# A two-block transformer on one core: Winograd's 2x2 products in a conv mixer, exchanged rope halves and scaled probabilities in attention, and other borders between stages

## The chip, the cores and the metric

One core of one Trainium2 chip. The metric is device time in microseconds of one launch, the median of three runs. TensorE runs at 1.2 or 2.4 GHz as the chip grants it; the profile calls full speed 1.0. Everything is computed in fp32. One fp32 matmul of the program is two MATMUL and two LDWEIGHTS instructions in the trace; a transpose is one of each.

## What is computed

The first block (windowed attention, a linear recurrence and a chunked RWKV part over 1024 tokens, with a layer norm) is not touched by the change. Behind it stands a second block of two layers over T = 1040 tokens (16 meta tokens and 1024) of width 1024:

```python
def short_conv_mixer(hn, w_in, conv_w, w_out):
    bcu = hn @ w_in                      # 1024 -> 3 x 1024
    b, c, u = jnp.split(bcu, 3, axis=-1)
    z = causal_conv(c * u, conv_w)       # 3 taps, each channel for itself
    return (b * z) @ w_out
# layer 0: h += short_conv_mixer(rmsnorm(h));  h += moe(rmsnorm(h))
# layer 1: cq = rmsnorm(rmsnorm(h) @ w_dq);  q = cq @ w_uq       (8 heads: 128 nope + 64 rope)
#          k_nope, v = rmsnorm(h' @ w_dkv) @ w_ukv;  k_rope shared by the heads
#          rope(x) = [x1 cos - x2 sin, x1 sin + x2 cos]
#          p = softmax(causal(q k^T * scale));  h += (p v) @ w_o;  h += moe(rmsnorm(h))
# out = rmsnorm(h) without the meta tokens
# moe: 8 groups x 8 experts, the two best experts of the best group for each token,
#      y = sum gate * (silu(x w_gate) * (x w_up)) w_down,  D_EXPERT = 256
```

## The kernel before

Each stage is one function with a `Phase` (L60 on), which owns buffers and semaphores, and in it one `nc.Block()`, in which each engine has its own written-out program; semaphores order them. A block ends with a DRAIN on each engine and a barrier. The exit of a phase (L76 on) clears the phase's semaphores and has another all-engine barrier (L80, L81). So nothing of the next stage begins before the slowest engine of the last is through. Order: `front`, the windowed attention, the RWKV chunks, `first_out`, `conv_mixer` (L1465), `back_and_route` and `experts` of layer 0 (both inside `moe`, L2750), `combine_and_latents` (L2376), `heads` (L1544), `moe` of layer 1, `combine_out` (L2650). `program_parts` (L2782) nests them. Weights of the next stage are loaded by SyncE (SP) at the end of a stage's program (`next_loads`).

`conv_mixer`: activations lie transposed, channels on partitions, as 8 k-tiles of 128 channels x 1040 tokens (`hnT`). For each of the 8 output tiles j and each of 3 cuts of the tokens (352, 352, 336) TensorE makes the three products b, c and u with 8 k-tiles each (L1505). ScalarE copies b and c out (L1520, L1521), VectorE multiplies c and u into z (L1533), and behind the last cut of a j come three taps (L1536, L1538) and the multiplication with b (L1541). TensorE is at most two cuts ahead of both (`z_made`, `copied`). Weights are 1.5 MB per j in a ring of two.

`heads` works on the 8 heads in 4 pairs. Per pair there are 14 projection jobs (L1665): four "qn" (nope of two heads x two halves of 512 tokens), "qa" and "qb" for the rope part of both heads (the same channels, in qb with the halves exchanged in the weights, made on the host), six "kn"; then the values (L1675). VectorE takes them out (L1820 to L1839): qa times cos (L1828), qb times sin (L1830), and their sum (L1831). Then 8 units of 128 query rows: scores (L1699, L1704), the mask and the largest (L1849 on), exp with its row sum on ScalarE (L1776), transposes of the probabilities ("turn", L1718), copies (L1789), and the product with the values ("mix", L1728). Probabilities are not normalised there: VectorE makes 1/sum and a diagonal of it (L1869, L1870), TensorE multiplies ones with that diagonal (L1730), which gives 1/sum of each query column on all partitions, and `output` copies this and multiplies (L1876, L1877). TensorE's order per unit is scores of unit n+1, then turn and mix of unit n, so that exp of n lies beside the scores of n+1.

`back_and_route` multiplies with W_out, adds, norms and routes the tokens; its GpSimd program gathers at its end the rows of the first two experts by indirect DMAs (L1256), behind all stores of hn. `experts` runs 32 pairs of experts per layer: gather (L2145), transposes (L1989), gate and up (L1996), silu and product, transposes, down (L2010), scatter of y rows to memory by indirect DMAs (L2150). SP streams the weights. `combine_and_latents` loads y rows of 3 tiles (L2418), scales its weights by the norm's gains on VectorE (L2606), and for each of 9 tiles makes h + gated y (`gathered_sum`, L2320, L2321), norms, turns and projects; `combine_out` does the sum and the last norm for 8 tiles.

## Time and profile before

| | us |
|---|---|
| median of 3 runs | 3064.82 (3064.04 to 3065.76) |
| the profiled execution | 3065.33 |
| its span | 3063.6 |
| mean granted clock of TensorE | 0.939 |

| stage | from | to |
|---|---|---|
| `conv_mixer` | 701.1 | 1045.2 |
| `back_and_route`, layer 0 | 1046.4 | 1230.0 |
| `experts`, layer 0 | 1230.7 | 1752.9 |
| `combine_and_latents` | 1755.0 | 1875.6 |
| `heads` | 1877 | 2323.6 |
| `experts`, layer 1 | 2489.9 | 3014.3 |
| `combine_out` | 3015.7 | 3063.6 |

Busy time of an engine counts the time in which it executes; what stands in brackets or behind a bar as idle is the time before an instruction, with the engine or DMA that ended it. A letter q behind an engine's name (POOLq, SPq) is its sequencer: waits, drains and DMA issues. L81 as a releaser is the barrier at a phase's exit.

### The profile page before, as it was taken

The numbers are of one execution on the slowest core, as the hardware profiler recorded it, in microseconds if no ns is written. First come the engines' busy times: TensorE is split into PE (matmuls) and PEld (weight loads), VectorE is DVE, ScalarE is ACT, GpSimd is POOL, SyncE is SP. The second block draws the span as 40 slices with busy tenths as digits, with TensorE's granted clock in tenths as the row PEclk, the third lists the DMA queues.
The fourth block names the chain that finished last, engine by engine and source line by source line (L and its number), as shares of the span: only waits on it lengthen the run. The fifth ranks groups of instructions, "written<-read, shape, count | busy, mean of one in ns | idle before, by whom it ended". The sixth has DMA issues, their size and how long they took to land. (4 is left out here: it accounts for less than half of the span.)

```text
span 3063.6 us, 36378 instructions
## 1 busy us (share of the span) xinstructions
PE 2695.4 (88%) x14806; PEld 1462.0 (48%) x14806; DVE 930.1 (30%) x2308; ACT 549.3 (18%) x1386; POOL 176.9 (6%) x255
## 2 busy tenths in 40 slices
PE   8999999998999898978787699999999978878872
PEld 3445579645666555323233265656665533323330
DVE  2414656452110145211011153434443432111114
ACT  0212455210000011111011131321221111111111
POOL 1000000000000000111111000000000011111110
PEclk9999999999999998999899899999999979988996
DMA  3111010221112045799999760020002469999995
GB/s 106 35 34 49 1 44 5 72 83 55 42 41 101 23 190 206 310 420 420 420 419 418 288 244 1 18 97 1 1 1 97 179 247 419 420 420 419 416 401 214
DMA packets 104937, 564.54 MB, mean 184 GB/s; under 512 B 20896, under 2 KB 21056, under 8 KB 52400
## 3 DMA queue, kind: packets, MB, share of 16 engines
q1 hardware_dynamic: 78432, 500.83, 40.8%
q0 software_dynamic: 21440, 43.51, 3.8%
q10 hardware_dynamic: 4896, 17.83, 1.4%
q8 instruction: 121, 1.98, 0.3%
q14 instruction: 48, 0.39, 0.0%
HBM read 529.84 MB, written 65.01 MB: 194 GB/s over the span
## 5 line engine op out<-in xcount | busy, mean ns | idle before, releaser
L1996 PE MATMUL ex__h_ps<-all__arena,ex__xT 128*64 128x512 f32 x1696 | 523.9, 670 | 172.8 <-DMA all__arena<-in_w_up 112.8
L1996 PEld LDWEIGHTS ex__h_ps<-all__arena,ex__xT 128*64 128x64 f32 x1696 | 169.3, 154 | 474.5 <-issue 470.1
L1505 PE MATMUL cm__acc<-all__arena,cw__w 128*128 128x352 f32 (+1 forms) x1152 | 338.0, 457 | 2.3 <-PEq L81 2.3
L287 PE MATMUL fr__acc<-X__xT,fr__w 128*128 128x512 f32 x640 | 280.8, 599 | 8.0 <-DMA X__xT<-in_xT 7.8
L1505 PEld LDWEIGHTS cm__acc<-all__arena,cw__w 128*128 128x128 f32 x1152 | 220.1, 191 | 120.0 <-issue 4.3
L1293 PE MATMUL pb__acc<-b__w,all__arena 128*128 128x512 f32 x544 | 244.8, 605 | 12.5 <-POOL pb__eps L1247 12.5
L2024 DVE TENSOR_TENSOR ex__hs<-ex__sg,ex__h_ps 128x256 f32<-128x256 f32 x64 | 27.0, 422 | 680.9 <-ACT ex__sg L2021 680.7
L287 PEld LDWEIGHTS fr__acc<-X__xT,fr__w 128*128 128x128 f32 x640 | 121.7, 192 | 164.7 <-issue 155.1
L1996 PE MATMUL ex__h_ps<-mo__wx,ex__xT 128*64 128x512 f32 x352 | 181.1, 674 | 0.0
L1293 PEld LDWEIGHTS pb__acc<-b__w,all__arena 128*128 128x128 f32 x544 | 102.7, 193 | 132.1 <-issue 118.4
L2010 PE MATMUL ex__y_ps<-b__w,ex__hT 128*64 128x512 f32 x672 | 153.5, 599 | 1.4 <-ACT ex__hT L2027 1.4
L2021 ACT ACTIVATE ex__sg<-ex__h_ps 128x256 f32<-128x256 f32 x64 | 24.5, 383 | 656.8 <-PE ex__h_ps L1996 656.8
L1728 PE MATMUL hd__o<-all__arena 128*128 128x128 f32 (+1 forms) x704 | 102.6, 286 | 4.0 <-ACT all__arena L1793 4.0
L2033 DVE COPY ex__ysb<-ex__y_ps 128x512 f32<-128x512 f32 x64 | 44.3, 692 | 189.7 <-PE ex__y_ps L2010 189.7
L1533 DVE TENSOR_TENSOR cm__z<-cm__cT,cm__acc 128x352 f32<-128x352 f32 (+1 forms) x24 | 12.4, 516 | 292.7 <-ACT cm__cT L1521 292.7
L2145 POOL DMA_INDIRECT b__rows<-s_hn,mo__queue x60 | 60.6, 1010 | 616.3 <-PE ex__x_ps L1989 608.5
L1728 PEld LDWEIGHTS hd__o<-all__arena 128*128 128x128 f32 (+1 forms) x704 | 88.1, 190 | 15.5 <-ACT all__arena L1793 7.5
L1989 PEld LDWEIGHTS ex__x_ps<-mo__ident,b__rows 128*128 128x128 f32 x512 | 63.2, 195 | 66.0 <-issue 66.0
L1989 PE MATMUL ex__x_ps<-mo__ident,b__rows 128*128 128x128 f32 x512 | 75.7, 292 | 15.4 <-PEq L81 15.4
L1665 PE MATMUL hd__s<-lt__cq,lt__wq 128*128 128x512 f32 x192 | 86.4, 609 | 2.8 <-POOL hd__ones L1639 2.8
L1060 PE MATMUL fo__acc<-all__arena 128*128 128x512 f32 x192 | 86.8, 602 | 1.9 <-PEq L81 1.9
L2010 PEld LDWEIGHTS ex__y_ps<-b__w,ex__hT 128*64 128x64 f32 x672 | 44.5, 136 | 78.6 <-issue 72.0
(417 smaller groups left out, 3506.5 us busy)
## 6 DMA issues: line engine op xcount, KB each, us to landing
all__arena<-in_w_gate SPq DMA_DIRECT2D x106, 1024.0 KB, 22.0
all__arena<-in_w_up SPq DMA_DIRECT2D x106, 1024.0 KB, 26.4
b__w<-in_w_down SPq DMA_DIRECT2D x84, 1024.0 KB, 20.7
all__arena<-in_w_down SPq DMA_DIRECT2D x22, 1024.0 KB, 16.9
mo__wx<-in_w_down SPq DMA_DIRECT2D x22, 1024.0 KB, 24.6
mo__wx<-in_w_gate SPq DMA_DIRECT2D x22, 1024.0 KB
mo__wx<-in_w_up SPq DMA_DIRECT2D x22, 1024.0 KB
all__arena<-s_ys SPq DMA_DIRECT2D x16, 1024.0 KB, 9.0
```

What stands on the lines that cost most here:

```text
L287: last = mm(acc[:, b, c], wbuf[:, b, k], xT[:, k, 512 * c:512 * c + 512], start=(k == 0), stop=(k == KT - 1))
L1060: last = nc.tensor.matmul(acc[:, t % 2, c], proj[:, G_T + k, P * t:P * t + P], wo[k][:, 512 * c:512 * c + 512], start=(k == 0), stop=(k == ...
L1293: last = mm(acc[:, t % 2, c], src[:, k, P * t:P * t + P], w[:, k, 512 * c:512 * c + 512], start=(k == 0), stop=(k == KT - 1))
L1505: last = nc.tensor.matmul(acc[:, u % 2, s, 0:cols], w[:, j % 2, s, k], hnT[:, k, at:at + cols], start=(k == 0), stop=(k == KT - 1))
L1665: last = mm(job_bank(n)[:, 0:cols], w[:, j % 2, k, which], src[:, k, at:at + cols], start=(k == 0), stop=(k == kt - 1))
L1728: mm(o_ps[:, h, 0:P], vv[0:r, s, h], pT[0:r, h, s], start=(a == 0), stop=(a == len(tiles) - 1))
L1989: last = nc.tensor.transpose(x_ps[:, k // 4, P * (k % 4):P * (k % 4) + P], xe[:, b, k::KT], ident[:])
L1996: last = nc.tensor.matmul(h_ps[half, b].rearrange("p (a b) -> p a b", a=2), xT[:, b, k, half], slots[n][:, :, k], start=(k == 0), stop=(k ...
L2010: last = nc.tensor.matmul(y_ps[half, c], hT[:, b, k, half], slots[n][:, k, 512 * c:512 * c + 512], start=(k == 0), stop=(k == 1))
L2024: return nc.vector.tensor_tensor(hs[:, b], sg[:, b], h_ps[:, b, DE:], ALU.mult)
L2033: return nc.vector.tensor_copy(ysb[:, b, 512:], y_ps[:, 1])
L2145: g.indirect_dma_start(xe[:, p % 2], None, hn_dram[:, :], bass.IndirectOffsetOnAxis(ap=queue[:, 0, p:p + 1], axis=0), bounds_check=T - 1, ...
```

## The change

Phases can be told that they lie `within` another: then they clear nothing at their own exit, and hand their semaphores to the outer one. The experts phases are within `moe`'s, and layer 0's `moe` within the phase around it.

```diff
+    def __init__(self, nc, name, within=None):
+
+        self.within = within
         again = Phase.seen[name] = Phase.seen.get(name, -1) + 1
...
-        if kind is None and self.sems:
+        if self.within is not None:
+            self.within.sems.extend(self.sems)
+        elif kind is None and self.sems:
 
             self.nc.clear_and_free_semaphores(self.sems)
             self.nc.all_engine_barrier()
```

`conv_mixer` computes its products by Winograd's form of Strassen's 2x2 scheme: two output tiles (m = 0, 1) and two halves of 520 tokens are the 2x2 result, two halves of the 1024 channels the inner dimension. There are 7 products with 4 k-tiles in place of 8, each of 260 columns (`TC`), for 4 pairs of output tiles x 3 sets (c, u, b) = 12 units, each in 2 chunks. Sums of weights and of activations before and of products after are made by VectorE; ScalarE only copies the first product. A unit's weights are 1 MB, in a ring of three; the first three units are loaded in `first_out`.

```diff
+        M1, M5, M6, M7, M2, M4, M3 = range(7)
+        U2, W, C22, V5, C11, C21, C12 = range(1, 8)
+        bank = lambda u, x: acc[:, (7 * u + x) % 8, 0:TC]
...
+                for n in range(3, NU):
+
+                    sp.wait_ge(product, 14 * (n - 2))
+                    conv_weight(sp, D, w, w_loaded, n)
...
                         if u >= 2:
-
-                            pe.wait_ge(z_made, u - 1)
-                            pe.wait_ge(copied, u - 1)
-                        for s in range(3):
-                            if u == 0:
-                                pe.wait_ge(part_loaded[s], 16)
-                            for k in range(KT):
-                                last = nc.tensor.matmul(acc[:, u % 2, s, 0:cols], w[:, j % 2, s, k],
-                                                        hnT[:, k, at:at + cols], start=(k == 0), stop=(k == KT - 1))
-                        last.then_inc(done, 1)
+                            pe.wait_ge(summed, 7 * (u - 2) + C12)
+                        mul(u, M1, a11, b11, c)
+                        pe.wait_ge(s_made, 4 * n + 1)
+                        pe.wait_ge(t_made, 4 * c + 1)
+                        if u:
+                            pe.wait_ge(e1_out, u)
+                        mul(u, M5, s1, t1, c)
+                        pe.wait_ge(s_made, 4 * n + 2)
+                        pe.wait_ge(t_made, 4 * c + 2)
+                        if u:
+                            pe.wait_ge(summed, 7 * (u - 1) + V5)
+                        mul(u, M6, s2, t2, c)
+                        pe.wait_ge(s_made, 4 * n + 3)
+                        pe.wait_ge(t_made, 4 * c + 3)
+                        mul(u, M7, s3, t3, c)
+                        mul(u, M2, a12, b21, c)
+                        if u:
+                            pe.wait_ge(summed, 7 * (u - 1) + C11)
+                        pe.wait_ge(t_made, 4 * c + 4)
+                        mul(u, M4, a22, t4n, c)
+                        if u:
+                            pe.wait_ge(summed, 7 * (u - 1) + C21)
+                        pe.wait_ge(s_made, 4 * n + 4)
+                        mul(u, M3, s4, b22, c)
```

VectorE's part: sums of weights (4 per unit, 512 elements), of activations (4 per chunk, once, 1040 elements), 7 per chunk of products (260 elements), and their order:

```diff
+                        v(V.tensor_tensor(sums[:, q, 0], a21, a22, ALU.add))
+                        dve.sem_inc(s_made, 1)
+                    if 2 in which:
+                        v(V.tensor_tensor(sums[:, q, 1], sums[:, q, 0], a11, ALU.subtract))
...
+                    V.tensor_tensor(out, a, b, op).then_inc(summed, 1)
+                    dve.wait_ge(summed, 7 * u + result)
...
+                    dve.wait_ge(e1_out, u + 1)
+                    dve.wait_ge(product, 7 * u + M6 + 1)
+                    add(u, U2, u2, e1[:, u % 2], bank(u, M6))
+                    dve.wait_ge(product, 7 * u + M7 + 1)
+                    add(u, W, c21, u2, bank(u, M7))
+                    add(u, C22, c22, c21, bank(u, M5))
+                    add(u, V5, c12, u2, bank(u, M5))
+
+                def last_sums(n, i, s, c):
+                    u = 2 * n + c
+                    c11, c12, c21, c22 = (dest(i, s, m, cols) for m in range(2) for cols in (low(c), high(c)))
+                    dve.wait_ge(product, 7 * u + M2 + 1)
+                    add(u, C11, c11, e1[:, u % 2], bank(u, M2))
+                    dve.wait_ge(product, 7 * u + M4 + 1)
+                    add(u, C21, c21, c21, bank(u, M4))
+                    dve.wait_ge(product, 7 * u + M3 + 1)
+                    add(u, C12, c12, c12, bank(u, M3))
...
+                    first_sums(nc_, i, 1, 0)
+                    if i == 0:
+                        row_sums(1, 1, 2, 3, 4)
+                    last_sums(nc_, i, 1, 0)
+                    weight_sums(nu, 1, 2, 3, 4)
+                    first_sums(nc_, i, 1, 1)
+                    last_sums(nc_, i, 1, 1)
+
+                    first_sums(nu, i, 2, 0)
+                    last_sums(nu, i, 2, 0)
+                    weight_sums(nb, 1, 2, 3, 4)
+                    first_sums(nu, i, 2, 1)
+                    last_sums(nu, i, 2, 1)
+                    gated(nu, i)
+                    if i == 0:
+                        dve.wait_ge(taps_loaded, 16)
+                    tap(i, 0, 0)
+
+                    first_sums(nb, i, 0, 0)
+                    tap(i, 0, 1)
+                    tap(i, 0, 2)
+                    last_sums(nb, i, 0, 0)
+                    if end:
+                        tap(i, 1, 0)
+                        tap(i, 1, 1)
```

`heads`: the rope jobs come first, "qb" is gone. The raw rope part is copied to `raw`, SP exchanges the halves into `rot` by four DMAs of 32 partitions, and VectorE does the rotation over all 1024 columns in three steps behind jobs 3 to 5. Probabilities are scaled before they are turned; the diagonals and the products with ones are gone.

```diff
-        jobs = ([("qn", h, c) for h in range(2) for c in range(2)] + [(kind, 0, c) for c in range(2) for kind in ("qa", "qb")]
+        jobs = ([("qr", 0, c) for c in range(2)] + [("qn", h, c) for h in range(2) for c in range(2)]
...
+                def exchange(j):
+
+                    sp.wait_ge(raw_out, 2 * (j + 1))
+                    for at in range(0, P, ROPE):
+                        for a, b in ((at, at + ROPE // 2), (at + ROPE // 2, at)):
+                            sp.dma_start(rot[a:a + ROPE // 2], raw[b:b + ROPE // 2]).then_inc(exchanged, 16)
+
+                exchange(0)
                 for j in range(2, NPAIR):
 
                     sp.wait_ge(pdone, NJ * (j - 1))
                     sp.wait_ge(v_done, NV * (j - 1))
                     pre.pair(sp, j)
+                    exchange(j - 1)
+                exchange(NPAIR - 1)
...
-                    pe.wait_ge(exped, 2 * u + h + 1)
+                    pe.wait_ge(normed, 2 * u + h + 1)
...
-                        mm(o_ps[:, h, 0:P], vv[0:r, s, h], pT[0:r, h, s], start=(a == 0), stop=(a == len(tiles) - 1))
-                    pe.wait_ge(diag_done, 2 * u + h + 1)
-                    mm(o_ps[:, h, P:2 * P], ones[:], dg[:, h, u % 2], start=True, stop=True).then_inc(mixed, 1)
+                        last = mm(o_ps[:, h, 0:P], vv[0:r, s, h], pT[0:r, h, s], start=(a == 0), stop=(a == len(tiles) - 1))
+                    last.then_inc(mixed, 1)
...
-                            v(tt(rot[:], job_bank(n), sinT[:, cols], ALU.mult))
-                            v.hold(tt(qr[:, cols], qr[:, cols], rot[:], ALU.add))
+                            v(V.tensor_copy(raw[:, cols], job_bank(n)))
...
+                def rotate(j, step):
+
+                    if step == 0:
+                        if j == 0:
+                            dve.wait_ge(tab_loaded, 32)
+                        v.hold(tt(qr[:], raw[:], cosT[:], ALU.mult))
+                    elif step == 1:
+                        dve.wait_ge(exchanged, 64 * (j + 1))
+                        v.hold(tt(rot[:], rot[:], sinT[:], ALU.mult))
+                    else:
+                        v(tt(qr[:], qr[:], rot[:], ALU.add))
...
                         v(V.reciprocal(rl[:, h, p:p + 1], ls[:, h, p, 0:1]))
-                        V.tensor_scalar(dg[:, h, p], ident[:], rl[:, h, p:p + 1], None, ALU.mult).then_inc(diag_done, 1)
+                        keys = keys_of(i)
+                        V.tensor_scalar(pr[:, h, p, 0:keys], pr[:, h, p, 0:keys], rl[:, h, p:p + 1], None,
+                                        ALU.mult).then_inc(normed, 1)
...
-                        v(V.tensor_copy(ob[:, h], o_ps[:, h, P:2 * P]))
-                        tt(oT[:, 2 * j + h, P * i:P * i + P], o_ps[:, h, 0:P], ob[:, h], ALU.mult).then_inc(oout, 1)
+                        V.tensor_copy(oT[:, 2 * j + h, P * i:P * i + P], o_ps[:, h, 0:P]).then_inc(oout, 1)
...
                         biggest(j, n)
+                        norms(j, n)
                         output(j, n - 1)
-                        diagonals(j, n)
```

The gathers of the first two experts move from the end of `back_and_route` to the beginning of `experts`; the first three y tiles of the stage behind are loaded by SP at the end of `experts`, when all scatters have been waited for:

```diff
-                pool.wait_ge(queue_done, 1)
-                for b in range(2):
-                    g.indirect_dma_start(hb[:, b], None, D["hn"][:, :],
-                                         bass.IndirectOffsetOnAxis(ap=queue[:, 0, b:b + 1], axis=0),
-                                         bounds_check=T - 1, oob_is_err=False).then_inc(x_loaded[b], 16)
...
-                next_loads(sp)
+                after.start(sp)
...
+                sp.wait_ge(scattered, 1)
+                after.first_rows(sp)
...
+                for b in range(2):
+                    gather(b)
...
+                pool.sem_inc(scattered, 1)
...
+    def rows_in(self, sp, t):
+        b, r = t % self.NBUF, rows_of(t)
+        sp.dma_start(self.yb[0:r, b], self.D["ys"][P * t:P * t + r]).then_inc(self.y_loaded[b], 16)
+
+    def first_rows(self, sp):
+        for t in range(self.NBUF):
+            self.rows_in(sp, t)
```

`combine_and_latents` loads only the later tiles itself; its weights are scaled by ScalarE (half before and half behind its first root) and GpSimd, no longer by VectorE. `combine_out` is changed in the same way without the scaling.

```diff
-                for t in range(NBUF):
-                    rows_in(t)
...
+                pool.wait_ge(g_loaded, 32)
+                pool.wait_ge(wk_loaded, 16)
+                for k in range(KT):
+                    nc.gpsimd.tensor_scalar(wk[:, k], wk[:, k], gains[:, 1, k:k + 1], None, ALU.mult).then_inc(k_scaled, 1)
...
+                def scale_q(first, last):
+                    for k in range(first, last):
+                        nc.scalar.activation(wq[:, k], wq[:, k], ACT.Copy, scale=gains[:, 0, k:k + 1]).then_inc(q_scaled, 1)
+
+                act.wait_ge(g_loaded, 32)
+                act.wait_ge(wq_loaded, 16)
+                scale_q(0, KT // 2)
                 roots(0)
+                scale_q(KT // 2, KT)
                 roots(1)
...
-                dve.wait_ge(g_loaded, 32)
-                for w, n, sem, ready in ((wq, 0, wq_loaded, q_scaled), (wk, 1, wk_loaded, k_scaled)):
-                    dve.wait_ge(sem, 16)
-                    for k in range(KT):
-                        v.hold(V.tensor_scalar(w[:, k], w[:, k], gains[:, n, k:k + 1], None, ALU.mult))
```

On the host, the fourth part of `w_uq_t` (the exchanged rope columns) is left out.

## Rows read from the trace of the kernel before

**Rows 1.** The page: busy time of the engines, and traffic in 40 slices.

```profile
PE 2695.4 (88%) x14806; PEld 1462.0 (48%) x14806; DVE 930.1 (30%) x2308; ACT 549.3 (18%) x1386; POOL 176.9 (6%) x255
...
GB/s 106 35 34 49 1 44 5 72 83 55 42 41 101 23 190 206 310 420 420 420 419 418 288 244 1 18 97 1 1 1 97 179 247 419 420 420 419 416 401 214
```

**Rows 2.** The windows: PE, PEld, DVE, ACT, POOL busy, granted clock, DMA share, GB/s.

```profile
1230.00:1240.00 10.00, 8.52 (x30) 3.62 (x32) 0.69 (x1) 1.87 (x2) 1.25 (x3) 0.61 0.09 26
1300.00:1400.00 100.00, 80.72 (x344) 31.17 (x340) 10.84 (x18) 10.97 (x24) 12.10 (x12) 0.90 1.02 420
1930.00:2330.00 400.00, 376.69 (x1913) 249.38 (x1914) 172.43 (x524) 95.92 (x296) 1.47 (x10) 0.99 0.05 19
620.00:640.00 20.00, 20.00 (x54) 9.32 (x53) 9.70 (x15) 3.19 (x7) 0.00 (x0) 1.00 0.52 184
```

**Rows 3.** The page's groups: busy us, mean ns, idle before them, what ended it.

```profile
L1996 PE MATMUL ex__h_ps<-all__arena,ex__xT 128*64 128x512 f32 x1696 | 523.9, 670 | 172.8 <-DMA all__arena<-in_w_up 112.8
...
L1505 PE MATMUL cm__acc<-all__arena,cw__w 128*128 128x352 f32 (+1 forms) x1152 | 338.0, 457 | 2.3 <-PEq L81 2.3
```

**Rows 4.** The timeline at the conv stage's start and end: start, duration, engine, line.

```profile
701.14 5.54 PE L1505 MATMUL cm__acc<-all__arena,cw__w 128*128 128x352 f32 x11 [2.26 <-PEq L81]
...
1043.96 1.24 DVE L1541 TENSOR_TENSOR all__arena<-all__arena,cm__bT 128x1040 f32<-128x1040 f32 x1
```

**Rows 5.** VectorE's groups, shapes apart.

```profile
L2320 DVE SCALAR_TENSOR_TENSOR all__arena<-all__arena,all__gate 128x1024 f32<-128x1024 f32 x17 | 21.8, 1283 | 8.1 <-DMA all__arena<-s_ys 6.5 <-DVE all__arena L2704 0.9 <-DVE all__arena L2321 0.4
...
L1541 DVE TENSOR_TENSOR all__arena<-all__arena,cm__bT 128x1040 f32<-128x1040 f32 x8 | 9.9, 1242 | 0.3
...
L1533 DVE TENSOR_TENSOR cm__z<-cm__cT,cm__acc 128x352 f32<-128x352 f32 x16 | 8.3, 522 | 188.6 <-ACT cm__cT L1521 188.6
...
L2571 DVE TENSOR_SCALAR all__arena<-all__arena,cl__rs 128x1024 f32<-128x1024 f32 x9 | 6.8, 754 | 0.3
```

**Rows 6.** The timeline of TensorE at a pair's change in heads.

```profile
1995.56 0.49 PE L1730 MATMUL hd__o<-hd__dg,hd__ones 128*128 128x128 f32 x2
...
1995.88 15.62 PE L1665 MATMUL hd__s<-lt__cq,lt__wq 128*128 128x512 f32 x36
...
2011.33 7.16 PE L1665 MATMUL hd__s<-lt__ckv,lt__wkv 128*128 128x352 f32 x24
```

**Rows 7.** The timeline of a unit in heads: exp, and the next turn.

```profile
1945.50 0.90 ACT L1776 ACTIVATE all__arena<-hd__s,hd__nm 128x784 f32<-128x784 f32 x1
...
1952.65 0.55 PE L1718 MATMUL hd__t<-hd__ident,all__arena 128*128 128x128 f32 x3
```

**Rows 8.** Instructions of three block ends: L2111, L1216, L2411, POOL's DRAIN.

```profile
L2111 POOLq DRAIN  x2: 5122/5124/5125, 1747.8 to 3009.2; - x2
...
L1216 POOLq DRAIN  x2: 4909/4958/5007, 1225.0 to 2484.1; - x2
...
L2411 POOLq DRAIN  x1: 797/797/797, 1836.8 to 1836.8; - x1
```

**Rows 9.** The timeline at the start of combine_and_latents and of combine_out.

```profile
1755.04 1.28 SPq L2418 DMA_DIRECT2D all__arena<-s_ys  x3
...
1760.75 1.29 DVE L2320 SCALAR_TENSOR_TENSOR all__arena<-all__arena,all__gate 128x1024 f32<-128x1024 f32 x1 [0.22 <-DVE all__arena L2606]
...
3015.66 1.27 SPq L2670 DMA_DIRECT2D all__arena<-s_ys  x3
...
3020.60 1.29 DVE L2320 SCALAR_TENSOR_TENSOR all__arena<-all__arena,all__gate 128x1024 f32<-128x1024 f32 x1 [4.81 <-DMA all__arena<-s_ys]
```

**Rows 10.** POOL's groups: its scaling by a column.

```profile
L498 POOL TENSOR_SCALAR V__bonus<-V__bonus,V__vec 128x1024 f32<-128x1024 f32 x2 | 5.7, 2847 | 0.1
```

**Rows 11.** The start of the experts: timeline, and the gathers of L1256.

```profile
1223.78 0.23 DVE L1462 COPY mo__total<-pb__lg_ps 128x64 f32<-128x64 f32 x1
...
1230.70 0.66 PE L1989 MATMUL ex__x_ps<-mo__ident,b__rows 128*128 128x128 f32 x2 [7.67 <-PEq L81]
...
DMA to landing us min/median/max: 3.6/3.8/4.1
```

More of the change, by code:

```diff
@@ L1166, in rows_of, with back_and_route @@
     return P if t < TT - 1 else LAST
-def back_and_route(nc, D, layer, tokens, src, h_in, h_out, keep, out, x_loaded, early, late):
+def back_and_route(nc, D, layer, tokens, src, h_in, h_out, keep, out, early, late):
     T, TT = tokens, -(-tokens // P)
@@ L2747, in start, with moe @@
         sp.dma_start(self.gb[:], self.D["norm_ffn_g_2"][self.layer].partition_broadcast(P)).then_inc(self.r_loaded, 16)
-def moe(nc, D, layer, tokens, src, out, h_out, gate, part, next_loads):
+def moe(nc, D, layer, tokens, src, out, h_out, gate, part, after, within=None):
     TT = -(-tokens // P)
-    with Phase(nc, "mo") as ph:
+    with Phase(nc, "mo", within) as ph:
         w, xe = out.w, out.rows
```

248 lines of the change are left out of this document (155 added, 93 removed).

## The prediction

> **What bounds the kernel now.** I read the page first, for which engine is full and where. TensorE is busy 2695 of 3064 us, and the row of GB/s shows the other limit: two plateaus near 420 GB/s [rows 1]. The windows tell the two apart. In the heads stage (1930 to 2330) TensorE is busy 376.7 of 400 us at clock 0.99 with a DMA share of 0.05, so there a matmul less is time less. In the experts stage (1300 to 1400) DMA stands at 1.02 and TensorE at 80.7 of 100, so there only an earlier start counts, and in its first ten microseconds DMA is at 0.09: the plateau has not begun [rows 2]. The groups of instructions say the same: the experts' first products idle 172.8 us, nearly all of it behind weight loads, while the conv mixer's 1152 instructions are 338.0 us busy with 2.3 us idle [rows 3]. The last view is the timeline at the stage borders, where every engine stands still: TensorE's own work decides conv and heads, a chain of waits decides the borders.
>
> **The conv mixer.** The stage runs from 701.14 to 1045.20 (start of the last multiply 1043.96 + 1.24) [rows 4], 344.06 us. Its products end at 701.14 + 338.0 = 1039.1, the tail after them is 6.1. A matmul instruction at full clock passes 1.2 columns per ns (two instructions per fp32 product): 36 of 512 columns take 15.45 us from start to start [rows 6], 429.2 ns each against 426.7 by columns, so 2.5 ns over. By columns the conv has 768 x 293.3 + 384 x 280 ns = 332.8 us; 11 instructions at the start took 5.54 instead of 3.23 us [rows 4], a loss of 2.3 at half clock, and the rest is again 2.5 ns each.
> After: 12 units x 2 chunks x 7 products x 4 k-tiles x 2 = 1344 instructions of 260 columns, 216.7 + 2.5 ns each: 294.6. The half-clock start stays, 2.3; VectorE's first sums (0.7 + 1.2) end within the first product's 3.5 us at that clock. The tail shrinks to one sum of 260 elements and a multiply over 2080 elements: VectorE takes 1.05 ns per element over 0.15 (352 in 0.522 us, 1040 in 1.242 [rows 5]), so 0.43 + 2.33 + about 0.3 of hand-over, 3.0. Stage 299.9: **-44.1**.
> What hides the new VectorE work: per stage 168 sums x 0.43, 48 weight sums x 0.69, 8 row sums x 1.24, 24 tap steps (0.76 to 1.30), 8 double multiplies x 2.33, together some 160 us, so 6.7 per chunk, and a chunk of TensorE is 56 x 0.219 = 12.3 us. I laid it out: with products of 1.75 us, VectorE finishes the first four sums at +8.4 and the others at +9.2, +10.9 and +12.6 us of a chunk, each before the product of the next chunk that waits for it; the weight sums of the next unit (2.8 us) fit a gap of 4.7. If that cover goes, each of the 168 groups pays. For the change of group alone the nearest row is the 128-column pair at 1995.56: 0.32 us instead of 0.213 [rows 6], so at most 0.107 each, +18.0; in the groups of six at 1995.88 it cost nothing, and I take nothing, since 8 instructions are nearer to six. Best end: no overhead and no slow start, -5.7. Range -26 to -50.
> Loads: 12 MB in 300 us, and 1.5 MB more in the stage before, where the load queued behind is awaited some 20 us later with DMA at a share of 0.52 [rows 2]: nothing.
>
> **The heads.** The second rope projection goes: 2 jobs x 6 instructions x 0.429 [rows 6] = 5.15 us per pair of heads, four pairs: **-20.6**. Its place is taken by four SBUF-to-SBUF DMAs per pair (128 KB in all four) that have 7.7 us or more until VectorE multiplies; VectorE gets two copies of 0.69 and three steps of 1.24, one behind each of the three qn jobs of 2.57 us. On SP the last exchange now stands ahead of the W_o loads; it is through early in pair 3, with 100 us left. The 64 ones x diagonal products go, 0.32 us each (1995.56 to 1995.88 [rows 6]): **-20.5**. In their place a turn waits for normed probabilities: a reciprocal (0.16) and a scaling of up to 1040 elements (0.75 for 1024 [rows 5]). In the row shown exp begins at 1945.50 and lasts 0.90, the turn starts at 1952.65 [rows 7]: 6 us for 2 x 0.95 on VectorE, because the next unit's scores lie between. Queued behind the new wait is `output`, whose result TensorE wants only one mix later. Cost nothing, but if that cover goes, up to the 0.65 us that a norm takes on the mean unit (0.16, and 0.49 for its 592 keys), 32 units: +20.9. Best end -43 (the copies of the output are shorter), worst -20. Value **-41.1**.
>
> **Ends of stages.** GpSimd's DRAIN takes 5.12 us at the end of the experts and 4.91 to 5.01 at the end of back_and_route, when the other engines are done; at the end of `combine_and_latents`, a block without indirect DMAs, it takes 0.80 [rows 8]. After the drain at 1747.8 + 5.12 = 1752.9 three phase exits last until 1755.04, 0.7 each.
> At `combine_and_latents` VectorE scales weights until 1760.75 [rows 9]. After: two exits less (-1.4), the scaling on ScalarE and GpSimd, rows in SBUF already: SP issues them at 1747.8, and the same loads land 4.94 us after issue (3015.66 to 3020.60 [rows 9]), at about 1752.7, under the drain. The first gather-sum starts at 1753.8: **-6.9**. ScalarE scales four tiles (about 0.5 each) before its first root, GpSimd its eight in about 0.9 each (2847 ns for 1024 columns [rows 10]), done near 1762, wanted after 1768.
> At `combine_out` the rows are there too and one exit is gone: 3020.60 becomes 3015.2, -5.4. Of 6.5 us that VectorE idles for y rows [rows 5], 1.7 come later; three rows less to carry there, so I take **-6.5**; bounds -5.4 and -7.1.
> At the start of the experts: without gathers the drain in back_and_route should go. VectorE's last copy ends at 1224.0, so the experts begin near 1225.1 instead of 1230.0, the end of the drain; the gathers are issued at 1225.8 and land after 3.6 to 4.1 us; the first turn comes at 1229.4 instead of 1230.70 [rows 11]: -1.3, and -1.1 in layer 1, **-2.4**. It counts in full since loads have not filled the queues yet [rows 2]. Bounds: 0 or, drain kept, +10.6.
>
> **Sum.** -44.1 - 41.1 - 6.9 - 6.5 - 2.4 = -101.0. The profiled execution took 3065.33 us (span 3063.6): 2964.3; the median of the runs is 0.5 lower, so **2964**.
>
> **Rivals.**
> A. Slower: conv products wait for VectorE's chain of sums. V5 and C11 free the banks of products of the next chunk, and if each product had to see two chained sums (2 x 0.43 us) end, 168 x 0.85 = +143: 3107. It decides from 101.0 / 168 = 0.60 us per group. For it: VectorE has twice the work it had. Against: 6.7 of 12.3 us. 3%.
> B. The change of group costs 0.107 us also with 260 columns: +18.0, 2982. Groups of only eight short instructions speak for it, those of six against. 12%.
> C. The drain belongs to the block and not to the gathers in it. Then the experts start at 1230.0 as now and the gathers come behind: 0.7 + 3.6 us, +4.3 instead of -1.2 per layer, +11: 2975. For it: the trace shows no end of this block without them; against: the 0.80 us of the third drain [rows 8]. 12%.
> D. Norms are exposed in the heads (price above): 2985. For it: VectorE carries 172 of 400 us there and TensorE idles 23 [rows 2]. 8%.
> E. GpSimd and VectorE, scaling and summing at once at the start of `combine_and_latents`, slow each other: if every one of VectorE's sums stands still during one GpSimd instruction of 0.9 us, 4 sums, +3.6: 2968. No row shows two SBUF inputs on VectorE beside GpSimd. 10%; inside my own range.
> The Trainium skill, "SBUF — State Buffer", section "Who interferes with whom", says that a VectorE instruction with two SBUF inputs and a GpSimd instruction share a port pair under an exclusive lock; by it E would happen, and without it nothing.
> The forecast itself, with E: 65%. Its own range is 2957 to 2970.
>
> **Range and chances.** The best ends of conv, heads and `combine_out` together would give 2964 - 5.7 - 1.9 - 0.6 = 2956, and I go 3 us lower for a norm or a wait that I see too dear: 2953, with 5% below. B, C and D reach 2985; mixtures of two of them lie higher, B with C at 2993, so I go to 2988 and leave them and A out. Range 2953 to 2988. Faster by over 0.2% (6 us, what a measurement can tell from none) in all but A: 0.95; between, 0.02; slower 0.03.
>
> **What would show it.** Conv: 1344 instructions in about 297 us, the idle before them under 5 us; idle released by VectorE would be A, a mean start distance of a group above 1.76 us B. Heads: pair length near 111 us; no idle before the turn released by VectorE. GpSimd's DRAIN at the end of back_and_route under 1 us, or C. The first gather-sum of `combine_and_latents` 0.9 us behind the experts' drain instead of 7.8. In `combine_out` no idle on y rows. I am wrong if conv or heads gives less than 35 us each.

## The result, and the profile after

The changed kernel takes **2973.5 us** (median of 4 runs, 2970.95 to 2975.03) where the kernel before takes 3065.29 (4 runs, 3064.04 to 3065.96): a ratio of 0.970, 95% interval 0.9683 to 0.9717. It is 91.8 us faster. The forecast was 2964, with 2953 to 2988 as its range: the range holds the time, the likeliest case's own range (2957 to 2970) misses it by 3.5 us. Rows are of executions with a span of 2973.0 (its time 2974.75) and, before, 3063.6 us. One launch of experiment 2 took 4623.8 us at a granted clock of 0.62 (the others show 0.94); it is in the median given there, and not in the ratio.

I cut both traces at the first product, or (`combine_and_latents`, `combine_out`) the first sum, of each stage. All differences in the text below are such distances.

| from the start of | to | before | after | difference | forecast |
|---|---|---|---|---|---|
| the program | conv | 701.14 | 703.18 | +2.04 | 0 |
| conv | `back_and_route`, layer 0 | 346.98 | 303.37 | -43.61 | -44.1 |
| `back_and_route` | `experts`, layer 0 | 182.57 | 181.21 | -1.36 | -1.3 |
| `experts` | `combine_and_latents` | 530.06 | 524.24 | -5.82 | -6.9 |
| `combine_and_latents` | `heads` | 116.56 | 116.54 | 0.0 | 0 |
| `heads` | `back_and_route`, layer 1 | 449.09 | 413.79 | -35.30 | -41.1 |
| `back_and_route` | `experts`, layer 1 | 163.53 | 163.61 | +0.1 | -1.1 |
| `experts` | `combine_out` | 530.66 | 524.95 | -5.71 | -5.4 |
| `combine_out` | the end | 42.95 | 42.13 | -0.82 | -1.1 |

The sum is -90.5 where -101.0 was forecast: the heads give 5.8 us less, the start costs 2.0, the conv is 0.5 and the borders together 2.2 off. The page after, its line of engines and two of its groups, which answer to [rows 1, 3]:

```profile
PE 2624.7 (88%) x14822; PEld 1477.7 (50%) x14822; DVE 1038.2 (35%) x2424; ACT 543.4 (18%) x1370; POOL 189.4 (6%) x262
...
L1521 PE MATMUL cm__acc<-all__arena,cw__w 128*128 128x260 f32 x576 | 136.0, 386 | 2.3 <-PEq L84 2.3
L1521 PE MATMUL cm__acc<-all__arena,cm__sums 128*128 128x260 f32 x576 | 134.6, 383 | 0.0
```

TensorE is 70.7 us less busy, VectorE 108 us more (it was 930.1), with the span 90.6 shorter: VectorE's extra work lies beside other work. No product of the conv mixer waits for it; the 2.3 us of idle time are the barrier ahead of the stage. Its start and end on the timeline (start, duration), against [rows 4]:

```profile
703.18 3.81 PE L1521 MATMUL cm__acc<-all__arena,cw__w 128*128 128x260 f32 x8 [2.26 <-PEq L84]
...
1000.50 0.43 DVE L1610 TENSOR_TENSOR cm__ub<-cm__ub,cm__acc 128x260 f32<-128x260 f32 x1 [1.33 <-PE cm__acc L1521]
1000.96 2.33 DVE L1694 TENSOR_TENSOR all__arena<-all__arena,cm__ub 128x2080 f32<-128x2080 f32 x1
```

From 703.18 to 1003.29 are 300.1 us, where 344.06 stood before and 299.9 was forecast. In the heads, the stretch that explains the miss is one unit's mix, up to the next scores. Before (timeline of TensorE, a unit in the third pair):

```profile
2153.66 2.42 PE L1728 MATMUL hd__o<-all__arena 128*128 128x128 f32 x18
2156.01 0.49 PE L1730 MATMUL hd__o<-hd__dg,hd__ones 128*128 128x128 f32 x2
2156.34 2.36 PE L1728 MATMUL hd__o<-all__arena 128*128 128x128 f32 x18
2158.63 0.49 PE L1730 MATMUL hd__o<-hd__dg,hd__ones 128*128 128x128 f32 x2
2158.95 1.45 PE L1699 MATMUL hd__s<-all__arena 128*128 128x512 f32 x3
```

And after, the same unit:

```profile
2082.40 4.82 PE L1887 MATMUL hd__o<-all__arena 128*128 128x128 f32 x36
2087.15 1.55 PE L1858 MATMUL hd__s<-all__arena 128*128 128x512 f32 x3
```

5.29 us from the mix to the scores became 4.75: 0.27 us for each ones x diagonal product taken away, where I had counted 0.32 from its start to the next start. (The view gives one shape per row; two of each 18 instructions are the meta tile's, 16 rows deep.) The 36 instructions that are left take 132 ns from start to start on the mean, not 113. The groups of this line after, shapes apart (busy, mean ns), show which ones are slow:

```profile
L1887 PE MATMUL hd__o<-all__arena 128*128 128x128 f32 x576 | 79.4, 283 | 4.0 <-ACT all__arena L1950 4.0
L1887 PE MATMUL hd__o<-all__arena 16*128 16x128 f32 x128 | 30.9, 321 | 0.0
```

Products with the meta tile, 16 rows deep, run longer than those 128 rows deep, although both pass 128 columns. Taken start by start, the trace says where: products 128 rows deep start 0.112 us apart. The first 16-row instruction starts 0.205 us behind its neighbour and the second 0.213 behind the first; the first 128-row one after them starts 0.200 us behind, and the next 0.213 behind that. Then it is 0.112 again. The first two stand, to 1 ns, at all 64 meta tiles of the stage, and the 0.200 at all but its last.

The borders, against [rows 8, 9, 11]. Instructions of two block ends after: GpSimd's DRAIN at the end of `back_and_route` and of the experts (least, median, most ns).

```profile
L1219 POOLq DRAIN  x2: 34/36/38, 1172.8 to 2391.0; - x2
...
L2277 POOLq DRAIN  x2: 5290/5290/5290, 1705.1 to 2924.5; - x2
```

The timeline after at the first products of the experts, the start of `combine_and_latents` and that of `combine_out`:

```profile
1187.77 1.97 PE L2155 MATMUL ex__x_ps<-mo__ident,b__rows 128*128 128x128 f32 x8 [6.42 <-DMA b__rows<-s_hn,mo__queue]
...
1705.06 1.28 SPq L2527 DMA_DIRECT2D all__arena<-s_ys  x3
...
1712.01 1.28 DVE L2491 SCALAR_TENSOR_TENSOR all__arena<-all__arena,all__gate 128x1024 f32<-128x1024 f32 x1 [11.18 <-PEq L84]
1712.25 1.19 POOL L916 TENSOR_SCALAR_AFFINE_SELECT cl__ident<-cl__ident 128x128 f32<-128x128 f32 x1 [0.15 <-POOL cl__ident L914]
...
1713.33 1.28 DVE L2492 SCALAR_TENSOR_TENSOR all__arena<-all__arena,all__gate 128x1024 f32<-128x1024 f32 x1
...
1713.48 12.06 POOL L2612 TENSOR_SCALAR all__arena<-all__arena,fw__gains 128x320 f32<-128x320 f32 x8
...
1716.16 1.43 DVE L2492 SCALAR_TENSOR_TENSOR all__arena<-all__arena,all__gate 128x1024 f32<-128x1024 f32 x1
...
1721.58 1.54 DVE L2491 SCALAR_TENSOR_TENSOR all__arena<-all__arena,all__gate 128x1024 f32<-128x1024 f32 x1
...
2930.89 1.28 DVE L2491 SCALAR_TENSOR_TENSOR all__arena<-all__arena,all__gate 128x1024 f32<-128x1024 f32 x1
```

The y rows are issued before the drain and are there after it, so the first sum starts 0.12 us behind the barrier instead of 5.7; GpSimd scales its eight tiles in 12.06 us beside VectorE's sums.

### The profile page after: what moved, and what is told of

Same layout as the page of the kernel before. It is cut to its first block and busy times, and to the rows that moved or that the text cites. A ratio compares the mean times of both kernels' runs of the same rounds, so it can differ in the third digit from the quotient of the medians.

```text
span 2973.0 us, 36737 instructions
## 1 busy us (share of the span) xinstructions
PE 2624.7 (88%) x14822; PEld 1477.7 (50%) x14822; DVE 1038.2 (35%) x2424; ACT 543.4 (18%) x1370; POOL 189.4 (6%) x262
## 5 line engine op out<-in xcount | busy, mean ns | idle before, releaser
L1521 PE MATMUL cm__acc<-all__arena,cw__w 128*128 128x260 f32 x576 | 136.0, 386 | 2.3 <-PEq L84 2.3
L1521 PE MATMUL cm__acc<-all__arena,cm__sums 128*128 128x260 f32 x576 | 134.6, 383 | 0.0
L1521 PEld LDWEIGHTS cm__acc<-all__arena,cw__w 128*128 128x128 f32 x576 | 110.4, 192 | 20.0 <-issue 2.9
L1521 PEld LDWEIGHTS cm__acc<-all__arena,cm__sums 128*128 128x128 f32 x576 | 110.0, 191 | 17.1
L2318 POOL DMA_INDIRECT s_ys<-ex__ysb,mo__queue x64 | 65.2, 1019 | 285.5 <-DVE ex__ysb L2199 285.5
```

The lines of the kernel that those rows point to most:

```text
L1521: last = nc.tensor.matmul(bank(u, x), weight(k), moving(k, c), start=(k == 0), stop=(k == HK - 1))
L2318: g.indirect_dma_start(y_rows[:, :], bass.IndirectOffsetOnAxis(ap=queue[:, 1, p:p + 1], axis=0), ysb[:, p % 2], None, bounds_check=2 * T - ...
```

## The experiments

Ten kernels, each the changed kernel with one thing undone or altered; a "distance" is a row of the table above. In brackets stands the ratio to the kernel before, measured beside it, with its 95% interval. The kernel before read 3067.5 us beside runs 1 to 4, 3068.5 beside 5 to 8 and 3069.3 beside 9 and 10, against 3065.3 beside the changed kernel, so medians of different runs compare to some 4 us only, and the distances are the finer measure. By then I had a theory of the missing 5.8 us in the heads: time is lost where the number of rows of consecutive products changes (meta tile 16, the others 128), the ones x diagonal products had only been carrying part of it, and what they cost themselves is two pitches of 0.112, 14.3 us in all. Its rivals: the price of 0.32 was right and the new code loses 6 us elsewhere (runs 2 and 3), or a product of 16 rows is slow by itself, whatever its neighbours (runs 4 and 5). The other runs try the terms of the sum that came as forecast, and the rivals on record.

**1. The old conv mixer put back, all else changed.** The whole function is exchanged; the comments here are added.

```diff
-def conv_mixer(nc, D, part, hnT, zT, w, w_loaded, next_loads):     # 7 products
+def conv_mixer(nc, D, hnT, zT, w, part_loaded, next_loads):        # the function of before
```

> The changed kernel with the conv mixer of the kernel before (576 products of 352 or 336 columns with 8 k-tiles, weights of 1.5 MB in a ring of two), all else as changed. If the conv stage gives its column work and nothing is taken back elsewhere, the stage is 344 us again and the time is 44 us above the changed kernel, near 3017. Rival: a share of the 44 us is lost in a neighbour (a later start of the conv stage, which began 2.1 us later in the changed kernel, or a lower granted clock behind it); then the difference is about 42 or less, and the conv stage starts at 701.1 again instead of 703.2.

Measured: 3018.82 us (0.9837, 0.9821 to 0.9854). The conv's distance is 347.60, 44.2 more than after; no other row moves by more than 0.6. The stage starts at 702.74 here too, 1.6 us later than before with the old conv's loads ahead of it, so a late start does not need the new ones.

**2. Diagonals and ones x diagonal products back, probabilities unscaled.**

```diff
-                    pe.wait_ge(normed, 2 * u + h + 1)
+                    pe.wait_ge(exped, 2 * u + h + 1)
...
-                    last.then_inc(mixed, 1)
+                    pe.wait_ge(normed, 2 * u + h + 1)
+                    mm(o_ps[:, h, P:2 * P], ones[:], dg[:, h, u % 2], start=True, stop=True).then_inc(mixed, 1)
...
-                        V.tensor_scalar(pr[:, h, p, 0:keys], pr[:, h, p, 0:keys], rl[:, h, p:p + 1], None, ALU.mult)
+                        V.tensor_scalar(dg[:, h, p], ident[:], rl[:, h, p:p + 1], None, ALU.mult)
```

> The changed kernel, only the normalisation as before: 1/sum as a diagonal, 64 products of ones with it, one copy and one multiplication per output. My prediction priced such a product at 0.32 us, so 20.5 us: near 2994. Theory now: the product itself costs two pitches of 0.112 us; the other 0.1 us was paid for changing from 16 active rows (the tile of the 16 meta tokens, last of the mix) to 128 rows, and whoever follows pays it. Then the time rises by 64 x 0.223 = 14.3 us to about 2988, and the heads stage is 425 us instead of 410.9.

Measured: 2990.31 us (0.9738, 0.9719 to 0.9758); heads 428.57, **+14.8**, that is 0.23 us per product. My price of 0.32 (20.5) is out; two instructions at their pitch of 0.112 (14.3) fit, to 0.5 us in all.

**3. The second rope projection back.**

```diff
-        jobs = ([("qr", 0, c) for c in range(2)] + [("qn", h, c) for h in range(2) for c in range(2)]
+        jobs = ([("qn", h, c) for h in range(2) for c in range(2)] + [(kind, 0, c) for c in range(2) for kind in ("qa", "qb")]
```

> The changed kernel, only the rope part by two projections as before (qa, qb) instead of the exchange by DMA. Predicted price of the 8 jobs: 8 x 2.57 = 20.6 us, near 2994, heads stage 431.5 us. Rival: the exchange by DMA costs something that the stage hides badly (a wait of VectorE for it, or the raw copies), then undoing it costs less than 20 us.

Measured: 2996.52 us (0.9764, 0.9747 to 0.978); heads 434.42, **+20.6**, the forecast to the tenth. With the last run this closes the account of the stage: 14.8 + 20.6 = 35.4 of 35.3.

**4. The meta tile's products made 128 rows deep** (rows 16 to 127 of its values and probabilities are zeroed once, and add nothing).

```diff
-    last = mm(o_ps[:, h, 0:P], vv[0:r, s, h], pT[0:r, h, s], start=(a == 0), stop=(a == len(tiles) - 1))
+    last = mm(o_ps[:, h, 0:P], vv[:, s, h], pT[:, h, s], start=(a == 0), stop=(a == len(tiles) - 1))
...
+                v.hold(V.memset(vv[:, NB], 0.0))
+                v(V.memset(pT[:, :, NB], 0.0))
```

> The changed kernel, but the products of the mix with the tile of the 16 meta tokens run over 128 rows: the rows 16 to 127 of that tile of the probabilities and of the values are zeroed once at the start of the stage. The output is the same. Theory of the changed rows: each mix now pays four pitches of 0.20 to 0.21 us instead of 0.112 (into the 16 rows, inside them, out of them, and the next), some 0.38 us too much; with 128 rows throughout this goes, 64 x 0.38 = 24 us less, near 2949, heads stage 387 us. Rival: what costs 0.1 us is the change of the accumulation group or of the PSUM bank behind a short product; then nothing changes, 2973, or it gets slower by the wider weight load.

Measured: **2949.02 us** (2948.68 to 2950.43; 0.9614, 0.9598 to 0.963), heads 390.19, **-23.6**. The same unit, with the same 36 instructions and 112 rows more in four of them, on TensorE's timeline:

```profile
2069.96 4.24 PE L1887 MATMUL hd__o<-all__arena 128*128 128x128 f32 x36
2074.04 2.80 PE L1858 MATMUL hd__s<-all__arena 128*128 128x512 f32 x8
```

And the group of all mixes in this kernel's stage:

```profile
L1887 PE MATMUL hd__o<-all__arena 128*128 128x128 f32 x704 | 86.1, 278 | 4.0 <-ACT all__arena L1950 4.0
```

4.08 us, 113 ns each: the excess over the pitch of 0.112 us is gone, and the mean of the group is below both of those after. This is the fastest version of the study, 24.5 us ahead of the changed kernel, by three lines.

**5. The two heads' meta tiles next to each other**, so that the number of rows changes twice per unit instead of four times, with the same products.

```diff
+                    if h == 1:
+                        tiles = tiles[-1:] + tiles[:-1]
```

> The changed kernel; head 1 of each mix takes its tile of 16 meta tokens first instead of last, so that it follows that of head 0. As many products of 16 rows as before, but two changes of rows per unit instead of four. If the change of rows is what costs 0.19 us, 32 x 2 x 0.19 = 12.2 us go: heads stage 398.7 us, time near 2961. If a product of 16 rows costs it by itself, wherever it stands, nothing changes: 410.9 and 2973.

Measured: 2962.82 us (0.9656, 0.9639 to 0.9674), heads 401.89, **-11.9**: half of run 4's, for half of the changes. A price of the 16-row product itself would have left the time alone. The unit on the timeline:

```profile
2077.59 4.63 PE L1889 MATMUL hd__o<-all__arena 128*128 128x128 f32 x36
2082.06 2.80 PE L1858 MATMUL hd__s<-all__arena 128*128 128x512 f32 x8
```

The group of the 16-row products in this kernel:

```profile
L1889 PE MATMUL hd__o<-all__arena 16*128 16x128 f32 x128 | 22.6, 296 | 0.0
```

4.47 us for the unit; the 16-row products' mean fell from 321 to 296 ns although nothing about them but their neighbours changed. Start by start, a 16-row product that follows another comes 0.112 us behind it, the pitch of the 128-row ones; 0.205 and 0.213 stand only where 16 rows follow 128, 0.200 and 0.213 only where 128 follow 16.

**6. The experts' first gathers back at the end of `back_and_route`.**

```diff
+                pool.wait_ge(queue_done, 1)
+                for b in range(2):
+                    g.indirect_dma_start(hb[:, b], None, D["hn"][:, :],
...
-                for b in range(2):
-                    gather(b)
```

> The changed kernel with the gathers of the first two experts at the end of back_and_route again. From the first product of W_out to the first turn of the experts the kernel before took 182.57 (layer 0) and 163.53 us (layer 1), the changed one 181.21 and 163.61. By my prediction the gathers bring the drain of 4.9 us back and both spans grow by 1.1 to 1.3; the traces so far show 0.1 to 1.4. If GpSimd's drain in back_and_route comes back to 4.9 us, it hangs on the indirect DMAs in the block. Rival: it hung on something else that the change took away, and stays at 0.04 us; then the spans get about 3 us shorter than in the changed kernel, since the gathers are issued earlier.

Measured: 2976.36 us (0.9699, 0.9682 to 0.9717). GpSimd's drain at the end of `back_and_route` is back:

```profile
L1219 POOLq DRAIN  x2: 4829/4914/4998, 1180.4 to 2402.1; - x2
```

The two distances are 182.39 and 165.10, +1.2 and +1.5: the drain belongs to the gathers, and rival C falls. The experts behind are longer too, by 2.1 and 0.5 us; what that is no row told me. GpSimd's drain at their end is shorter, 5.12 us as in the kernel before, where the changed kernel and the nine others have 5.29.

**7. The first three y tiles loaded in their own stage.**

```diff
-                sp.wait_ge(scattered, 1)
-                after.first_rows(sp)
...
+                pre.first_rows(sp)
```

> The changed kernel; the first three tiles of y rows are loaded at the start of combine_and_latents and of combine_out again. The first sum then waits for the landing, 4.9 us after the stage starts, instead of 0.1: the first sums come 4.8 us later each, +9.6 in all, and in combine_out up to 1.1 more for later loads: +10, time near 2983. Rival: the rows loaded during the experts' drain lengthen that drain (5.29 instead of 5.12 us), so that undoing it costs 0.3 less.

Measured: 2983.0 us (0.9722, 0.9705 to 0.9739). Distances +5.2 and +4.9 at the experts' ends and +0.7 to the end, 10.8 in all.

**8. All the scaling of weights in `combine_and_latents` back on VectorE.**

```diff
-                for k in range(KT):
-                    nc.gpsimd.tensor_scalar(wk[:, k], wk[:, k], gains[:, 1, k:k + 1], None, ALU.mult)
...
+                for w, n, sem, ready in ((wq, 0, wq_loaded, q_scaled), (wk, 1, wk_loaded, k_scaled)):
...
+                        v.hold(V.tensor_scalar(w[:, k], w[:, k], gains[:, n, k:k + 1], None, ALU.mult))
```

> The changed kernel; in combine_and_latents VectorE scales all weights again ahead of its first sum (16 operations, 5.2 us), ScalarE and GpSimd none. The y rows are loaded early as in the changed kernel. The first sum comes 5.4 us later and everything behind it: +5.4. Rival (GpSimd's reads slow VectorE's sums, which took up to 1.54 instead of 1.28 us while GpSimd needed 1.5 instead of 0.9 us for a tile): then VectorE gets back some 0.8 us, and the whole costs +4.6 or less.

Measured: 2978.16 us (0.9709, 0.9692 to 0.9726). The distance to the stage's first sum is 530.44, +6.2, and that from there to `heads` 116.75, +0.2: more than either expectation, and no sign that VectorE gets time back that reaches the heads. The first of the two sums of a tile, beside an idle GpSimd (groups of VectorE in this stage):

```profile
L2491 DVE SCALAR_TENSOR_TENSOR all__arena<-all__arena,all__gate 128x1024 f32<-128x1024 f32 x9 | 11.5, 1280 | 0.4 <-DVE all__arena L2783 0.2 <-DVE all__arena L2492 0.2
```

The same group in the changed kernel, and GpSimd's scaling beside it:

```profile
L2491 DVE SCALAR_TENSOR_TENSOR all__arena<-all__arena,all__gate 128x1024 f32<-128x1024 f32 x9 | 11.8, 1307 | 11.4 <-PEq L84 11.2 <-DVE all__arena L2492 0.2
...
L2612 POOL TENSOR_SCALAR all__arena<-all__arena,fw__gains 128x320 f32<-128x320 f32 x8 | 12.1, 1522 | 0.0
```

**9. Each phase clears its own semaphores again.**

```diff
-        if self.within is not None:
-            self.within.sems.extend(self.sems)
-        elif kind is None and self.sems:
+        if kind is None and self.sems:
```

> The changed kernel with an exit of its own for each phase again (no `within`): three exits between the experts and combine_and_latents, two ahead of combine_out. By my prediction an exit costs 0.7 us, so 3 x 0.7 = +2.1 us. The changed trace shows 1.6 us from the end of the drain to the first sum with one exit, where the kernel before had 2.1 with three: if a merged exit clears what three did, each one left out is worth only 0.3, and the whole +0.8.

Measured: 2975.04 us (0.9698, 0.9678 to 0.9718), by the time no different from the changed kernel (0.970). In the trace the exits are there: from the end of the experts' drain to the first sum 2.39 us instead of 1.62 in layer 0, and 1.8 instead of 1.1 in layer 1, 1.5 in all. That lies between the two expectations: merging three exits into one saves 0.8, not the forecast's 1.4. The one that is left clears all their semaphores; that this takes the rest is likely, but no run separates it.

**10. Eight needless sums more on VectorE in each of the conv's 24 chunks.**

```diff
                     add(u, C12, c12, c12, bank(u, M3))
+                    for _ in range(8):
+                        v(V.tensor_tensor(u2, u2, u2, ALU.subtract))
```

> The changed kernel; VectorE makes eight more operations of 260 elements (0.43 us each, 3.4 us) behind the sums of each of the 24 chunks of the conv mixer, on data that nobody needs. If VectorE has the spare time of my sum (6.7 of 12.3 us per chunk), 10.1 are still below 12.3 and the conv stage stays at 300 us; a tail of 3.4 us comes at the end, since the last chunk's extra work stands ahead of the last multiplication: +3.4. If the products hang on VectorE's chain of sums (rival A), each chunk grows by a part of the 3.4 us, up to 24 x 3.4 = 82 us.

Measured: 2979.83 us (2975.41 to 2983.12; 0.9714, 0.9697 to 0.973); the profiled execution has a conv distance of 307.08, **+3.7**. The window over the stage (busy PE, PEld, DVE, ACT, POOL; granted clock, DMA share, GB/s) of this kernel:

```profile
700.00:1005.00 305.00, 297.11 (x1344) 256.63 (x1344) 243.05 (x450) 9.02 (x24) 0.00 (x0) 0.99 0.15 52
```

And of the changed one:

```profile
703.00:1003.00 300.00, 297.21 (x1344) 256.79 (x1344) 160.55 (x258) 9.04 (x24) 0.00 (x0) 0.99 0.15 52
```

82 us more on VectorE, half as much again, and the products take the same. What came is the last chunk's eight sums ahead of the last multiply, on VectorE's timeline:

```profile
998.51 3.67 DVE L1635 TENSOR_TENSOR all__arena<-all__arena 128x260 f32<-128x260 f32 x8
1002.21 2.33 DVE L1696 TENSOR_TENSOR all__arena<-all__arena,cm__ub 128x2080 f32<-128x2080 f32 x1
```

The median moved by 2.6 us more than the conv; its runs spread over 7.7 us, the kernel before read 4.0 us more beside it than beside the changed kernel, and I read nothing into the rest.

## Why the prediction came out as it did

**Conv, right.** -43.6 for -44.1, and not by terms that cancel: the products took 297.2 us of 296.9 forecast with the slow start, the tail behind them 2.9 of 3.0. Column count over 1.2 per ns plus 2.5 ns held for a shape that the trace of before did not have. The cover for VectorE was larger than it had to be (run 10), so rival A (3%) never was near. Rival B's price of a change of group, read from the 128-column pair in [rows 6], does not exist here: the stage took 300.1 us. What that pair showed was something else, below.

**Heads, the mechanism right, one term mis-sized.** The rope projection was -20.6 and measured 20.6. The 64 diagonal products were "0.32 us each", -20.5, and measured 14.8. The step that failed is to take an instruction's price from its start to its neighbour's start. The 0.32 us hold two instructions at 0.112 and 0.1 that is paid because the product before was 16 rows deep and this one 128. Taken away, the product leaves that 0.1 to whatever stands behind: the next mix, or the scores, whose second instruction starts 0.53 us behind the first instead of 0.43. 64 x 0.1 = 6.4 us, which covers the 5.8 that the stage gave too little. Runs 4 and 5 show it from both sides: two changes of depth per unit cost 4.47 - 4.08 = 0.39 us, four 4.75 - 4.08 = 0.67 up to the scores' start and that 0.1 behind it, none 0; so 0.19 each. Over the stage it is the same: 23.6 us for 128 changes, 11.9 for 64. I had the clue in the rows: 0.32 in [rows 6] where 36 products of 512 columns came to 2.5 ns over their columns, and I kept it as a bound for the conv instead of asking why it was there.

Norms in the turn's way (rival D) did not come: TensorE's waits in this stage are those of before, almost to the tenth. The view of TensorE's waits before (us in total, times, longest):

```profile
PE hd__t L1718 <- ACT all__arena L1789: 8.8, 20, 0.6
PE hd__t L1718 <- ACT all__arena L1793: 4.0, 8, 0.7
```

And after:

```profile
PE hd__t L1877 <- ACT all__arena L1946: 8.9, 20, 0.6
PE hd__t L1877 <- ACT all__arena L1950: 4.1, 8, 0.7
```

One mark that I set was wrong by itself: "pair length near 111 us" is the length before (110.5 from one pair's first kn job to the next). 41.1 less over four pairs makes 100; it is 101.9, by the 8.8 us per pair that 35.3 makes. And the four DMAs of a pair move 128 KB each, 512 in all four, not 128; they land in 2.3 to 3.6 us, so the cover of 7.7 us held all the same.

**Borders.** The first border of the experts came as forecast (-1.36 for -1.3), in layer 1 nothing came (+0.1 for -1.1); but that stage's length moves between 161.8 and 163.7 us in the other kernels of this study, which leave it alone, and run 6 gives +1.5 there. In layer 0 it moves too, between 180.0 and 181.6, so the agreement there to a tenth is in part luck. At the end of layer 0's experts two exits less were to save 1.4 us and saved 0.6 (from the drain's end at 1710.4 to 1711.89 are 1.5 us, 2.1 before), and the drain is 0.17 longer, which goes with the two gathers moved into this block (run 6): -5.8 for -6.9. The first sum starts 1.62 us behind the drain, where the sign on record was 0.9. `combine_out` was -6.53 for -6.5. Rival C is refuted by the drain of 36 ns and by run 6. Its price was counted too high: gathers issued at 1230.7 and landed 3.6 us later give 1234.3, which is +3.6 against the first turn at 1230.70, not +4.3.

Rival E happened and cost nothing. Three of VectorE's sums beside GpSimd's scaling take 1.43 to 1.54 us instead of 1.28. A scaling of GpSimd takes 1.52 on the mean: 1.08 for the two with no sum beside them, where the rows of before had let me expect 0.9, and 1.49 to 2.10 for the others. Yet the distance to `heads` stayed at 116.54, since the weights are wanted only after the first tiles. Nor is it a full stop of a sum for one scaling, for which I had 0.9 us. The Trainium skill, "SBUF — State Buffer", section "Who interferes with whom", says the two share a port pair under an exclusive lock. The trace agrees that they meet, and it is mostly GpSimd that pays: VectorE loses 0.15 to 0.26 us in three sums and nothing in the others, GpSimd 0.4 to 1.0 us in six scalings. The nearest to waiting out a whole instruction is GpSimd's L916: 1.19 us beside a sum, ending 0.15 us behind the sum's end, where the same instruction (L913) took 0.34 in this stage before.

**The 2 us ahead of the conv** were counted as nothing. The first block's window from 100 to 200 us has TensorE at a granted clock of 0.98, where it was 1.00 before, and the stage behind that block starts at 327.08 instead of 325.06: all of the 2 us. The window before:

```profile
100.00:200.00 100.00, 100.00 (x232) 43.54 (x231) 32.57 (x25) 24.19 (x20) 0.00 (x0) 1.00 0.11 36
```

And after:

```profile
100.00:200.00 100.00, 100.00 (x229) 43.42 (x228) 32.57 (x25) 24.20 (x20) 0.00 (x0) 0.98 0.11 36
```

In the eleven kernels with the change the conv starts anywhere from 700.3 to 705.0 us, while this block is the same in all. It is not always lost in this stretch: in run 1 the window stands at 1.00 and the stage behind starts at 324.9, and 1.8 us are lost after it. It is a matter of the execution, not of the change, and of the size that a forecast of a kernel like this has to leave room for.

## What to carry to other kernels

Before pricing an instruction by the distance to its neighbour's start, ask what of that distance its neighbour causes: compare it with the same shape in a long row of its kind, and where it stands above, expect the excess to stay when the instruction goes. On TensorE keep the depth of consecutive products equal, unless shallow products lie in different rows and run side by side, as the scores' rope products do here; a ragged K tile padded with zeros to 128 rows was worth 24 us here, more than the 64 products that the change took away. And test a cover by doubling the load: one run with 82 us of needless sums settled what a page of hand-made timing had only argued.

## What the runs showed of the hardware

- A change of depth between consecutive 128-column fp32 products costs 0.19 us, half of it ahead of the first instruction behind the change and half between that and the next: 4.75, 4.47 and 4.08 us for the same 36 instructions with four, two and no changes. The Trainium skill, "TensorE: Matmul & The Clock Gate", section "The mechanism", says that "LDWEIGHTS overlaps with in-flight MATMULs only when row_grp differs". The trace does not agree for products in the same rows: 128 rows behind 128 rows start 0.112 us apart (106.7 ns by their 128 columns) although each weight load takes 0.19 us, so the loads do overlap; the extra time stands where 16 rows and 128 rows, which share rows, meet. It agrees for different rows: the scores' rope products are 64 rows deep, one head's in rows 0 to 63 and the other's in 64 to 127, and in the changed kernel two of them start 6 to 7 ns apart (2089.98 us), two in the time of one. They pay for the change behind the 128-row products too (0.32 us from start to start where 0.23 stood, then 0.53 where 0.43 did), but padded to 128 rows they would share rows; it was not tried.
- GpSimd's DRAIN at a block's end takes 4.8 to 5.3 us in the blocks whose program issues indirect DMAs, and 36 ns in `back_and_route` when they were moved out of it. They are not its only cause: at the end of the first block's program, which issues plain DMAs only, it takes 4.50 us in the kernel before. What the five microseconds are spent on stays open: in the experts it takes 5.29 us with the y rows loaded before it and without, and 5.12 where the first two gathers are in another block (before the change, and run 6).
- A phase exit has no fixed price: three took 2.1 us before (2.3 in run 9), the single one that clears all their semaphores 1.5.
- VectorE's sums with two SBUF inputs and GpSimd's scalings slow each other down: 1.28 to 1.43 and 1.54 us on the one side, 1.08 to between 1.49 and 2.10 on the other.
